# A hybrid attention layer: the differential mixer's output normalized on VectorE, its heads 2 and 3 written in place

## The chip, the cores and the metric

One NeuronCore of one Trainium2 chip runs the whole kernel. The metric is the device time of one execution in microseconds (us). Engines: PE is TensorE (matmul), DVE is VectorE, ACT is ScalarE, POOL is GpSimd, SP is the sync engine, which issues all DMAs here.

## What is computed

One layer on a sequence of 1024 tokens of 1024 features, all in float32. The normalized input is projected to queries, keys and values of two mixers; both mixers' outputs (8 rows of 128 features) are concatenated and projected back; then come a gated convolutional FFN, a gated per-layer input and a last norm. The change is in the second mixer and in the output projection behind it. Cut to that:

```python
for blk in range(s // Q_BLOCK):            # 8 blocks of 128 queries, for each of 4 heads
    sc = einsum('bqhmd,bkhmd->bhmqk', q[:, qs:qe], k[:, :qe]) * HEAD_DIM ** -0.5
    sc = where(allowed, sc + bias, NEG_INF)   # keys up to the block's end: 128, 256, ... 1024
    pr = softmax(sc)
    a = pr[:, :, 0] - lam * pr[:, :, 1]       # two maps m = 0, 1 a head
    outs.append(einsum('bhqk,bkhe->bqhe', a, v[:, :qe]))
o = rms_norm(concatenate(outs), subln_g) * (1.0 - lambda_init)
h = h + concatenate([oa, ob]) @ w_out
```

## The kernel before

Every operand of a matmul is held as a high part and a low part (tensor minus high part), and each product is three matmuls (`SPLIT3`). ACT writes the high part, then DVE writes the low part by a subtraction (`low`, L781; on the profile's lines L513 and L783).

The stages follow one another: input norm and value projection, seven units of the query and key projection, mixer A with further units between its blocks (to 214 us), mixer B, `oproj`, FFN, last stage. All engines run hand-written streams in program order, held together by semaphores.

**Mixer B** is 32 blocks, m = 8 times head plus query block; m mod 8 = i gives a width of w = 128(i + 1) keys. The loop over n (L1292 on PE, L637 on ACT, L976 on DVE, L480 on POOL) is a software pipeline: in turn n, PE issues

- the scores of block n (`b_score`, L1223), after the exponentials of block n-1 (they share their PSUM banks);
- the product with the values of block n-2 (L1295), after its low part (`b_tlo`);
- in turns 28 to 34 a `c_unit`;
- the turn of the finished output of block n-3 (L1317, PSUM bank 7), after `b_y` and after `b_part` of block n-2, which uses the same bank;
- the turn of the probabilities of block n-1 (L1325), after their difference (`b_diff`);
- a filler: half of a projection unit (12 matmuls of 512 columns), in turns 1 to 20. Two halves make a unit, whose result ACT and DVE split (`unit_hi`, `unit_lo`), and which now and then is followed by the split of a further weight tile;
- from turn 26 on a `c_unit` at the end: 9 matmuls that apply `C_ROWS` = 3 of the 8 rows of `w_out` to one half tile of the output; DVE adds it to h (`c_add`, L917).

ACT in turn n: `b_part` of n-2 (L645: both halves of the product, 256 columns, from PSUM, scaled), the copy of the turned output of n-3 (`b_yhi`), the high part of the turned probabilities of n-1 (`b_thi`), the two exponentials of n (`b_exps`, L583), the square of the output of n-2 (L665), then `fill_hi` and `wo_hi` (split of rows of `w_out`).

DVE in turn n: the difference of n-1 (`b_diffs`, L883), the logits of n (`b_logits`, L896: a minimum over the keys farther than 256, then two bias-and-minimum passes), `b_ylo` of n-3, `b_tlo` of n-1, `fill_lo`, `wo_low`, with `c_add` between.

POOL per block (L480 to L494): adds the halves of the product, takes the power of the mean square, scales the output (L491), multiplies by the gain (L494, `b_y`).

SP writes each of the 32 turned outputs to DRAM (`mix_b`) and reads them back as rows 4 to 7 of `act_t`; it also loads `w_out`, mixer A's rows and the residual. After turn 34 PE waits for all 16 `c_unit`s to be added and for `b_ylo` of block 31, and runs `oproj` (L1354) with the 5 remaining rows for 8 tiles.

```python
                pe.wait_ge(S.b_y, m + 1)                     # L1313, m = n - 3
                pe.wait_ge(S.b_part, min(m + 2, NBS))
```

Of the kernel before, what the change touches and what calls it, by code (L numbers as in the profile page):

```python
# [63 lines left out]
def build(nc, x, p, w_in, w_out, sinks, lambda_q, lambda_k, subln_gain, rel_bias, norm_mix, norm_ffn,  # L64
# [57 lines left out]
    y_t = bias_a[:, 0, 0, :]  # L122
# [26 lines left out]
    wp = wbuf[:, 6 * D:10 * D].rearrange("p (l k n) -> p l k n", l=2, k=KP)  # L149
    pt = wbuf[:, 0:D].rearrange("p (s l n) -> p s l n", s=2, l=2)  # L150
# [8 lines left out]
    b_scores b_max b_exp b_diff b_turned b_thi b_tlo b_pv b_part b_sum b_sq b_y b_yturned b_yhi b_ylo  # L159
    wo_hi wo_lo mix_c mix_3 mix_456 mix_7 c_done c_added oproj h_mid sq1 ms1 pow1 xs1_ready tr1 xhi1 xlo1 gffn_in  # L160
# [44 lines left out]
    C_TWO = C_FROM + 2 * (NBS + 3 - C_FROM) - 2 * NT  # L205

    def c_mid(n):
        return C_TWO - C_FROM + 2 * (n - C_TWO) if n >= C_TWO else None

    def c_end(n):  # L210
        return c_mid(n) + 1 if n >= C_TWO else n - C_FROM if n >= C_FROM else None

    def c_bank(c):
        return c % 2 if c > c_mid(NBS) else 0


    WO_SPLITS = {24: (0,), 25: (1, 2), NBS: (3,), NBS + 1: (4, 5), NBS + 2: (6,)}
# [47 lines left out]
    def _(sp):  # L265
# [97 lines left out]
        def load_wo(k):  # L363
            if k >= 3:
                sp.wait_ge(S.wo_lo, k - 2)
            sp.dma_start(raw[:, k % 3, :], w_out[k * P:(k + 1) * P, :]).then_inc(raw_loaded[k % 3], 16)

        for n in range(NBS):
# [5 lines left out]
            if n == 18:  # L374
                sp.wait_ge(S.a_pv, NA)
                sp.wait_ge(S.unit_done, NUNIT)
                for k in range(3):
                    load_wo(k)
            if n == 19:
                sp.wait_ge(S.a_stored, 16 * NA)  # L380
                mix_a_back(0, S.mix_c)
                mix_a_back(1, S.mix_c)
            if n == 20:
                mix_a_back(2, S.mix_c)
                sp.wait_ge(S.w_lo, NTILE)
# [69 lines left out]
        sp.wait_ge(b_stored[0], 16 * (NBS // 2))  # L455
        sp.wait_ge(b_stored[1], 16 * (NBS // 2))
# [3 lines left out]
    def _(pool):  # L460
# [19 lines left out]
        for n in range(NBS):  # L480
            o, st = o_t[:, :], 16 + 3 * (n % 2)
            pool.wait_ge(S.b_part, n + 1)
            if n >= 1:
                pool.wait_ge(S.b_y, n)
            nc.gpsimd.tensor_tensor(o, o_sb[:, 0, :], o_sb[:, 1, :], ALU.add).then_inc(S.b_sum, 1)
            pool.wait_ge(S.b_sq, n + 1)
            link(nc.gpsimd.tensor_scalar(stat[:, st + 1:st + 2], stat[:, st:st + 1], 1.0 / P, EPS, ALU.mult, ALU.add))
            link(nc.gpsimd.tensor_tensor(stat[:, st + 2:st + 3], stat[:, st + 1:st + 2], stat[:, 63:64], ALU.pow))
            if n == 0:
                pool.wait_ge(S.consts_scaled, 1)  # L490
            link(nc.gpsimd.tensor_scalar(o, o, stat[:, st + 2:st + 3], None, ALU.mult))  # L491
            if n >= 1:
                pool.wait_ge(S.b_yturned, n)
            nc.gpsimd.tensor_tensor(y_t[:, :], o, g_sub[:, :], ALU.mult).then_inc(S.b_y, 1)  # L494
# [16 lines left out]
    def _(act):  # L511
# [984 lines left out]
```

## Time and profile before

| what | value |
|---|---|
| median of 3 runs | 1411.56 us (1409.98 to 1412.71) |
| the profiled execution's own time | 1411.1 us |
| its span, first to last instruction | 1409.3 us |
| mean granted TensorE clock | 0.979 |
| PE busy | 1325.0 us (94%) |
| DVE, ACT, POOL busy | 801.3, 405.7, 127.9 us |
| mixer B, first score to last turn | 205 to 458 us of the span |
| `oproj` | 458.6 to 527 us |

A busy share is that of the whole span. Where the order of the streams matters, the timeline is the view to read: it lists instructions of one or all engines in order of time, with the idle time before each and what ended it.

### The profile page before, as it was taken

How to read it: one execution, taken by the hardware profiler on the slowest of the kernel's cores; microseconds unless marked ns; L12 is line 12 of the kernel's file. 1: busy time of each engine (PE TensorE's matmuls, PEld its weight loads, DVE VectorE, ACT ScalarE, POOL GpSimd, SP SyncE). 2: the span in 40 equal slices, each digit the busy share in tenths (PEclk: the TensorE clock that was granted, in tenths of full speed). 3: DMA queues.
4: the chain of work that ended last, by engine and by line, in shares of the span. 5: the costliest groups of instructions: out<-in, count | busy, mean ns of one | idle time of the engine just before them, and what ended most of it. 6: DMA issues, size and time to landing. Idle time of an engine off the chain costs nothing.

```text
span 1409.3 us, 17050 instructions
## 1 busy us (share of the span) xinstructions
PE 1325.0 (94%) x6451; PEld 1074.7 (76%) x6451; DVE 801.3 (57%) x1316; ACT 405.7 (29%) x792; POOL 127.9 (9%) x205
## 2 busy tenths in 40 slices
PE   4999998888689999999999999999999999979997
PEld 4987876666567787888888888888888888857775
DVE  3424776675575453555666666666556655584443
ACT  4323655554343222111111111111221111123321
POOL 0000002434343000000000000000000000040000
PEclk9999999999689999999999999999999999999999
DMA  6462331100745312111111111111111112121111
GB/s 186 83 113 45 83 83 42 49 19 20 179 138 160 113 31 72 52 56 46 45 45 45 45 45 45 45 45 45 45 45 45 45 46 69 57 90 48 42 38 45
DMA packets 107453, 91.11 MB, mean 65 GB/s; under 512 B 12818, under 2 KB 96522, under 8 KB 107338
## 3 DMA queue, kind: packets, MB, share of 16 engines
q1 hardware_dynamic: 107402, 90.43, 23.0%
q8 instruction: 33, 0.54, 0.2%
q14 instruction: 18, 0.15, 0.0%
HBM read 74.49 MB, written 14.94 MB: 63 GB/s over the span
## 4 chain that ended last, share of the span: by engine, by line
PE 63%; DVE 3%; issue 2%; ACT 1%; POOL 0%; POOLq 0%; ACTq 0%; DVEq 0%
PE ps L1143 62%; DVE h L1068 1%; PE ps L1153 1%; DVE wbuf L783 1%; DVE xs L1099 0%; POOL o_t L491 0%; ACT wbuf L513 0%; DVE conv L1041 0%; DVE conv L1051 0%; DVE conv L1046 0%; PE ps L1412 0%; DVE h L921 0%; DVE gel L1134 0%; ACT L768 0%; DVE conv L1122 0%
## 5 line engine op out<-in xcount | busy, mean ns | idle before, releaser
L1143 PE MATMUL ps<-act_t,wbuf 128*128 128x512 f32 x2496 | 592.2, 398 | 6.0 <-DVE wbuf L783 3.7
L1143 PEld LDWEIGHTS ps<-act_t,wbuf 128*128 128x128 f32 x2496 | 470.3, 189 | 123.3 <-DVE wbuf L783 8.1
L1068 DVE TENSOR_TENSOR h<-ps,h 128x512 f32<-128x512 f32 x352 | 238.4, 690 | 199.7 <-PE ps L1143 199.7
L1143 PE MATMUL ps<-wbuf 128*128 128x512 f32 x1152 | 271.4, 393 | 8.8 <-DVE h L1068 8.8
L1143 PEld LDWEIGHTS ps<-wbuf 128*128 128x128 f32 x1152 | 216.8, 189 | 56.7 <-DVE h L1068 10.1
L1143 PE MATMUL ps<-act_t,wq 128*128 128x512 f32 x624 | 157.1, 404 | 0.8 <-DVE wq L785 0.7
L1143 PEld LDWEIGHTS ps<-act_t,wq 128*128 128x128 f32 x624 | 115.8, 191 | 26.8 <-issue 1.1
L783 DVE TENSOR_TENSOR wbuf<-raw,wbuf 128x1024 fp32r<-128x1024 f32 x75 | 87.9, 1220 | 41.4 <-ACT wbuf L678 34.0
L714 ACT ACTIVATE gel<-conv 128x1024 f32<-128x1024 f32 x22 | 23.3, 1060 | 293.1 <-DVE conv L1051 293.1
L513 ACT ACTIVATE a_buf<-ps 128x1024 f32<-128x1024 f32 x22 | 22.6, 1028 | 267.0 <-PE ps L1143 267.0
L1143 PE MATMUL ps<-wbuf,act_t 128*128 128x512 f32 x336 | 85.9, 407 | 3.1 <-DVE h L921 3.0
L499 POOL TENSOR_TENSOR act_t<-raw,act_t 128x1024 fp32r<-128x1024 f32 x6 | 16.7, 2797 | 720.8 <-ACT act_t L513 720.8
L1143 PEld LDWEIGHTS ps<-wbuf,act_t 128*128 128x128 f32 x336 | 62.6, 191 | 18.7 <-DVE h L921 4.6
L678 ACT ACTIVATE wbuf<-raw 128x1024 fp32r<-128x1024 f32 x66 | 64.8, 1044 | 0.0
L1143 PE MATMUL ps<-wq,act_t 128*128 128x384 f32 (+1 forms) x384 | 59.5, 315 | 0.3 <-DVE act_t L783 0.3
L1143 PEld LDWEIGHTS ps<-wq,act_t 128*128 128x128 f32 x384 | 57.8, 193 | 0.7 <-DVE act_t L783 0.7
L783 DVE TENSOR_TENSOR a_t<-ps,a_t 128x512 fp32r<-128x512 f32 (+4 forms) x64 | 44.6, 716 | 22.7 <-ACT a_t L513 22.3
L1143 PE MATMUL ps<-wq 64*128 64x512 f32 (+3 forms) x288 | 38.1, 391 | 14.0 <-ACT e_t L592 13.6
L592 ACT ACTIVATE e_t<-ps,small 128x128 f32<-128x128 f32 (+7 forms) x64 | 46.7, 738 | 5.7 <-DVE small L908 5.6
L1143 PEld LDWEIGHTS ps<-wq 64*128 64x128 f32 x288 | 25.8, 203 | 28.6 <-ACT e_t L592 14.6
L513 ACT ACTIVATE a_t<-ps 128x512 fp32r<-128x512 f32 (+4 forms) x64 | 38.0, 618 | 31.7 <-DMA mix_a<-a_t 12.9
L1143 PEld LDWEIGHTS ps<-v_b,a_t 128*128 128x128 f32 x288 | 40.0, 213 | 8.1 <-issue 5.8
(120 smaller groups left out, 1083.4 us busy)
## 6 DMA issues: line engine op xcount, KB each, us to landing
raw<-in_w_ffn_in SPq DMA_DIRECT2D x44, 512.0 KB, 5.0
raw<-in_w_ffn_out SPq DMA_DIRECT2D x22, 512.0 KB, 5.8
w_raw<-in_w_in SPq DMA_DIRECT2D x10, 512.0 KB, 4.6
x_in<-in_x SPq DMA_DIRECT2D x8, 512.0 KB, 3.3
mix_a<-a_t SPq DMA_DIRECT2D x16, 256.0 KB, 3.0
mix_b<-mst SPq DMA_DIRECT2D x32, 128.0 KB, 1.7
raw<-in_w_out SPq DMA_DIRECT2D x8, 512.0 KB, 5.1
act_t<-mix_a SPq DMA_DIRECT2D x16, 256.0 KB, 5.1
```

Of the source, the lines that this page charges most:

```text
L499: nc.gpsimd.tensor_tensor(act_t[:, 1, r, :], raw[:, (KD + r) % 3, :], act_t[:, 0, r, :].bitcast(F32), ALU.subtract).then_inc(S.wg_lo, 1)
L513: nc.scalar.activation(dst, src, ACT.Copy, scale=scale).then_inc(done, 1)
L592: nc.scalar.activation(e_t[:, pr, m, 0:w], psf[:, at:at + w], ACT.Exp, scale=-1.0, bias=small[:, o + 2 + m:o + 3 + m], accum_out=small[:, ...
L678: ins = nc.scalar.activation(wf[:, s, 0, j, :], raw[:, j, :], ACT.Copy)
L714: nc.scalar.activation(gel[:, :], conv[:, :], ACT.Gelu).then_inc(S.gelu_done, 1)
L783: ins = nc.vector.tensor_tensor(dst, src, hi.bitcast(F32), ALU.subtract)
L1068: nc.vector.tensor_tensor(h[:, t, sl], ps[:, 4 + g % 4, :], h[:, t, sl], ALU.add).then_inc(S.h_add, 1)
L1143: return nc.tensor.matmul(dst, lhs, rhs, start=start, stop=stop)
L1153: ins = nc.tensor.transpose(psf[:, bank * HALF + k * P:bank * HALF + (k + 1) * P], src[:, k * P:(k + 1) * P], ident[:, :])
```

## The change

It moves work and order in mixer B, and rows between the two parts of the output projection:

- the output of a block is no longer scaled and multiplied by the gain on POOL. ACT copies and scales one half of the product to `o_t` (`b_half`), DVE adds the other half in one pass (`b_part`), ACT squares the sum, POOL only computes the power (`b_pow`), and DVE applies power and gain in one pass (`y`, one turn later);
- on ACT, `b_thi` now serves block n-2 and stands first, `b_yhi` serves n-4, and the half of the product of n-2 and its square stand behind the exponentials of n. On DVE, `b_tlo` of n-2 and `b_ylo` of n-4 stand first, then the difference of n-1, the logits of n, y of n-3, `b_part` of n-2;
- on PE the turn of the probabilities of n-1 stands ahead of the turn of the output of n-3, whose waits are the same; the filler follows, in turns 0 to 19; there are 36 turns;
- heads 2 and 3 (blocks 16 to 31) are written straight into `act_t` and not by way of DRAM;
- `C_ROWS` is 2: a `c_unit` has 6 matmuls, stands at the end of the turn, one in turns 22 to 31, two in turns 32 to 34; `oproj` has 6 rows a tile. `w_out` is split in another order, and some tiles lie elsewhere in memory.

```diff
     def b_fill(n):
-        return NA + 1 + n if 1 <= n < HALVES - NA - 1 else None
+        return NA + 2 + n if n < HALVES - NA - 2 else None
-    C_ROWS = 3
-    C_FROM = 26
+    C_ROWS = 2
+    C_FROM = 22
+    VIA_DRAM = 2 * NT
+    def c_units(n):
+        if n < C_FROM:
+            return ()
+        if n < NBS:
+            return (n - C_FROM,)
+        first = NBS - C_FROM + 2 * (n - NBS)
+        return tuple(c for c in (first, first + 1) if c < 2 * NT)
-    WO_SPLITS = {24: (0,), 25: (1, 2), NBS: (3,), NBS + 1: (4, 5), NBS + 2: (6,)}
+    O_ROWS = (4, 5, 6, 2, 3, 7)
+    WO_ORDER = (0, 1) + O_ROWS
+    WO_SPLITS = {20: (0,), 21: (1,), 25: (2,), 26: (3,), NBS: (4,), NBS + 2: (5,), NBS + 3: (6,)}
...
+        sp.wait_ge(S.unit_done, NUNIT)
+        mix_a_back(0, S.mix_c)
+        mix_a_back(1, S.mix_c)
...
+        for j in range(3, KD):
+            load_wo(j)
+            if j == 5:
+                sp.wait_ge(S.c_done, 2 * NT)
+                mix_a_back(2, S.mix_23)
+                mix_a_back(3, S.mix_23)
...
         for n in range(NBS):
-            o, st = o_t[:, :], 16 + 3 * (n % 2)
-            pool.wait_ge(S.b_part, n + 1)
-            if n >= 1:
-                pool.wait_ge(S.b_y, n)
-            nc.gpsimd.tensor_tensor(o, o_sb[:, 0, :], o_sb[:, 1, :], ALU.add).then_inc(S.b_sum, 1)
+            st = 16 + 3 * (n % 2)
             pool.wait_ge(S.b_sq, n + 1)
+            if n >= 2:
+                pool.wait_ge(S.b_y, n - 1)
             link(nc.gpsimd.tensor_scalar(stat[:, st + 1:st + 2], stat[:, st:st + 1], 1.0 / P, EPS, ALU.mult, ALU.add))
-            link(nc.gpsimd.tensor_scalar(o, o, stat[:, st + 2:st + 3], None, ALU.mult))
-            nc.gpsimd.tensor_tensor(y_t[:, :], o, g_sub[:, :], ALU.mult).then_inc(S.b_y, 1)
...
-        for n in range(NBS + 3):
+        for n in range(NBS + 4):
             if 2 <= n <= NBS + 1:
                 m = n - 2
-                nc.scalar.activation(o_sb[:, :, :], ps[:, 7, 0:2 * P].rearrange("p (a q) -> p a q", a=2), ACT.Copy,
-                                     scale=small[:, col:col + 1]).then_inc(S.b_part, 1)
...
                 copy(a_t[:, 0, 0:w], psf[:, 5 * HALF:5 * HALF + w], S.b_thi)
+            if n >= 4:
+                m = n - 4
+                act.wait_ge(S.b_yturned, m + 1)
+                copy(mix_dst(m, 0), ps[:, 7, 3 * P:4 * P], S.b_yhi)
             if 2 <= n < NBS:
                 b_exps(n)
             if 2 <= n <= NBS + 1:
                 m = n - 2
+                act.wait_ge(S.b_pv, m + 1)
+                if m >= 1:
+                    act.wait_ge(S.b_part, m)
+                act.wait_ge(S.b_diff, m + 1)
+                nc.scalar.activation(o_t[:, :], ps[:, 7, 0:P], ACT.Copy,
+                                     scale=small[:, col:col + 1]).then_inc(S.b_half, 1)
+                act.wait_ge(S.b_part, m + 1)
+                square(o_sb[:, m % 2, :], sq_out, stat[:, 16 + 3 * (m % 2):17 + 3 * (m % 2)], S.b_sq)
             fill_hi(b_fill(n))
...
+        for n in range(NBS + 4):
+            if 2 <= n <= NBS + 1:
+                m = n - 2
                 w = P * (m % NT + 1)
                 dve.wait_ge(S.b_thi, m + 1)
                 low(a_t[:, 1, 0:w], psf[:, 5 * HALF:5 * HALF + w], a_t[:, 0, 0:w], S.b_tlo)
+            if n >= 4:
+                m = n - 4
+                dve.wait_ge(S.b_yhi, m + 1)
+                low(mix_dst(m, 1), ps[:, 7, 3 * P:4 * P], mix_dst(m, 0), S.b_ylo)
+            if 2 <= n <= NBS:
+                b_diffs(n - 1)
+            if 2 <= n < NBS:
+                b_logits(n)
+            if 3 <= n <= NBS + 2:
+                m = n - 3
+                dve.wait_ge(S.b_pow, m + 1)
+                nc.vector.scalar_tensor_tensor(out=y_t, in0=o_sb[:, m % 2, :], scalar=stat[:, st + 2:st + 3],
+                                               in1=g_sub[:, :], op0=ALU.mult, op1=ALU.mult).then_inc(S.b_y, 1)
+            if 2 <= n <= NBS + 1:
+                m = n - 2
+                dve.wait_ge(S.b_half, m + 1)
+                nc.vector.scalar_tensor_tensor(out=o_sb[:, m % 2, :], in0=ps[:, 7, P:2 * P],
+                                               scalar=small[:, col:col + 1], in1=o_t[:, :],
+                                               op0=ALU.mult, op1=ALU.add).then_inc(S.b_part, 1)
             fill_lo(b_fill(n))
+            for c in c_units(n):
+                c_add(c)
...
                 ins.then_inc(S.b_turned, 1)
+            if 3 <= n <= NBS + 2:
+                m = n - 3
+                pe.wait_ge(S.b_y, m + 1)
+                pe.wait_ge(S.b_part, min(m + 2, NBS))
+                if m >= 1:
+                    pe.wait_ge(S.b_ylo, m)
+                nc.tensor.transpose(ps[:, 7, 3 * P:4 * P], y_t, ident[:, :]).then_inc(S.b_yturned, 1)
             if b_fill(n) is not None:
                 unit(FIRST_UNITS + b_fill(n) // 2, b_fill(n) % 2)
-            if c_end(n) is not None:
-                c_unit(c_end(n))
+            for c in c_units(n):
+                c_unit(c)
```

## Rows read from the trace of the kernel before

**Rows 1.** Busy time by stretch: us, PE, PEld, DVE, ACT, POOL, PE clock, DMA.

```profile
300.00:340.00 40.00, 35.21 (x212) 27.47 (x211) 24.57 (x62) 20.64 (x60) 16.50 (x30) 1.00 0.06 20
380.00:420.00 40.00, 32.36 (x165) 24.78 (x166) 25.90 (x62) 19.00 (x55) 17.27 (x27) 0.77 0.40 137
```

**Rows 2.** Timeline of all engines, turn 14 (start, us, instruction, idle before).

```profile
301.20 1.49 PE L1143 MATMUL ps<-wq 64*128 64x512 f32 x12
301.64 1.02 DVE L892 SCALAR_TENSOR_TENSOR e_t<-e_t,small 128x768 f32<-128x768 f32 x1
302.62 1.36 PE L1143 MATMUL ps<-v_b,a_t 128*128 128x256 f32 x10
302.76 1.49 DVE L903 TENSOR_REDUCE small<-ps 128x2 f32<-128x1280 f32 x1
303.18 0.61 POOL L491 TENSOR_SCALAR o_t<-o_t,stat 128x128 f32<-128x128 f32 x1
...
304.02 0.47 ACT L645 ACTIVATE o_sb<-ps,small 128x256 f32<-128x256 f32 x1 [2.59 <-PE ps L1143]
304.29 0.49 DVE L908 CUSTOM_DVE_ANT_0 ps<-ps,bias_b,small 128x256 f32<-128x256 f32 x1
...
304.60 0.30 PE L1317 MATMUL ps<-ident,bias_a 128*128 128x128 f32 x1 [0.61 <-POOL bias_a L494]
...
304.73 0.83 PE L1325 MATMUL ps<-ident,e_t 128*128 128x128 f32 x6
...
305.32 3.05 PE L1143 MATMUL ps<-act_t,wq 128*128 128x512 f32 x12
305.60 0.81 ACT L513 ACTIVATE a_t<-ps 128x768 fp32r<-128x768 f32 x1 [0.39 <-PE ps L1325]
306.31 1.00 ACT L592 ACTIVATE e_t<-ps,small 128x896 f32<-128x896 f32 x1
306.45 0.96 DVE L783 TENSOR_TENSOR a_t<-ps,a_t 128x768 fp32r<-128x768 f32 x1 [0.92 <-ACT a_t L513]
...
308.44 1.65 PE L1143 MATMUL ps<-wq 64*128 64x512 f32 x12
...
308.57 0.60 ACT L513 ACTIVATE wq<-ps 128x512 fp32r<-128x512 f32 x1
...
309.20 0.69 DVE L785 SCALAR_TENSOR_TENSOR wq<-ps,wq 128x512 fp32r<-128x512 f32 x1 [1.79 <-ACT wq L513]
```

**Rows 3.** Groups of instructions, whole span: busy us, mean ns of one, idle before.

```profile
L1317 PE MATMUL ps<-ident,bias_a 128*128 128x128 f32 x32 | 10.1, 316 | 19.2 <-POOL bias_a L494 11.2 <-issue 7.3 <-ACT o_sb L645 0.7
L783 DVE TENSOR_TENSOR mst<-ps,mst 128x128 fp32r<-128x128 f32 x32 | 9.2, 287 | 12.8 <-ACT mst L513 12.2
L516 ACT ACTIVATE o_sb<-o_t 128x128 f32<-128x128 f32 x32 | 10.0, 312 | 0.0
```

**Rows 4.** Timeline of PE: turns 1, 3, 21 and 26, and the start of `oproj`.

```profile
217.65 0.47 PE L1325 MATMUL ps<-ident,e_t 128*128 128x128 f32 x1 [2.89 <-DVE e_t L892]
217.78 4.52 PE L1143 MATMUL ps<-act_t,wq 128*128 128x512 f32 x12
...
226.36 0.97 PE L1143 MATMUL ps<-wq 64*128 64x512 f32 x6
...
347.31 1.32 PE L1143 MATMUL ps<-wq 64*128 64x512 f32 x12
...
394.30 2.91 PE L1143 MATMUL ps<-wbuf,act_t 128*128 128x512 f32 x6
...
458.61 21.52 PE L1143 MATMUL ps<-wbuf,act_t 128*128 128x512 f32 x90 [0.85 <-DVE h L921]
```

**Rows 5.** Timeline of all engines after the last exponential (block 31).

```profile
436.15 0.21 ACT L592 ACTIVATION_READ_ACCUMULATOR e_t<-ps,small 128x1 f32 x1
...
452.03 2.71 POOL L491 TENSOR_SCALAR o_t<-o_t,stat 128x128 f32<-128x128 f32 x1
```

**Rows 6.** The page's DMA issues: size of each, median us from issue to landing.

```profile
act_t<-mix_a SPq DMA_DIRECT2D x16, 256.0 KB, 5.1
```

More of the change, by code:

```diff
@@ L361, in residual, with load_wo @@
             sp.dma_start(h[:, t, :], x[t * P:(t + 1) * P, :]).then_inc(x_again[t], 16)
[L363 to L368, printed above, removed]
+        def load_wo(j):
+            k = WO_ORDER[j]
+            if j >= 3:
+                sp.wait_ge(S.wo_lo, j - 2)
+            sp.dma_start(raw[:, j % 3, :], w_out[k * P:(k + 1) * P, :]).then_inc(raw_loaded[j % 3], 16)
+        for n in range(VIA_DRAM):
             sp.wait_ge(S.b_ylo, n + 1)
@@ L677, in f_split_hi @@
                     continue
[L678 removed]
+                ins = nc.scalar.activation(wf[:, 1 - s, 0, j, :], raw[:, j, :], ACT.Copy)
             ins.then_inc(S.f_hi, 1)
@@ L887, in b_diffs @@
             dve.wait_ge(S.b_exp, 2 * m + 2)
+            if m >= 2:
+                dve.wait_ge(S.b_part, m - 1)
             link(nc.vector.reciprocal(small[:, o + 12:o + 14], small[:, o + 8:o + 10]))
@@ L974, in _ @@
                 b_logits(1)
-        for n in range(NBS + 3):
-            if 2 <= n <= NBS:
-                b_diffs(n - 1)
-            if n > C_FROM:
-                c_add(c_end(n - 1))
-            if 2 <= n < NBS:
-                b_logits(n)
-            if c_mid(n) is not None:
-                c_add(c_mid(n))
-            if 3 <= n:
-                m = n - 3
-                dve.wait_ge(S.b_yhi, m + 1)
-                low(mst[:, m % 2, 1, 0:P], ps[:, 7, 3 * P:4 * P], mst[:, m % 2, 0, 0:P], S.b_ylo)
-            if 1 <= n <= NBS:
-                m = n - 1
+        for n in range(NBS + 4):
+            if 2 <= n <= NBS + 1:
+                m = n - 2
                 w = P * (m % NT + 1)
@@ L1290, in _ @@
                 unit(FIRST_UNITS + a_fill(n) // 2, a_fill(n) % 2)
-        for n in range(NBS + 3):
+        for n in range(NBS + 4):
             if 2 <= n < NBS:
@@ L1308, in _ @@
                 ins.then_inc(S.b_pv, 1)
-            if c_mid(n) is not None:
-                c_unit(c_mid(n))
-            if n >= 3:
-                m = n - 3
-                pe.wait_ge(S.b_y, m + 1)
-                pe.wait_ge(S.b_part, min(m + 2, NBS))
-                if m >= 1:
-                    pe.wait_ge(S.b_ylo, m)
-                nc.tensor.transpose(ps[:, 7, 3 * P:4 * P], y_t[:, :], ident[:, :]).then_inc(S.b_yturned, 1)
             if 1 <= n <= NBS:
@@ L1364, in oproj @@
                         ins = mm(ps[:, 2 * (t % 2) + half, :], act_t[:, a, k, t * P:(t + 1) * P],
-                                 wo(k)[:, b, HALF * half:HALF * (half + 1)],
-                                 k == C_ROWS and n == 0, k == KD - 1 and n == 2)
-            if rows[-1] == KD - 1:
+                                 wo(k, b)[:, HALF * half:HALF * (half + 1)],
+                                 k == O_ROWS[0] and n == 0, k == O_ROWS[-1] and n == 2)
+            if rows[-1] == O_ROWS[-1]:
                 ins.then_inc(S.oproj, 1)
```

182 lines of the change are left out of this document (75 added, 107 removed).

## The prediction

> **What bounds the kernel now.** I read the busy time by stretch first. In a stretch of mixer B with fillers PE is busy 35.2 of 40 us at the full clock of 2.4 GHz; later, without fillers, it is busy 32.4 of 40 us at a granted 0.77, part of it at the lower level of 1.2 GHz [rows 1]. Then the timeline of one turn, 14 (i = 6), says what closes the loop. From one score to the next are 7.24 us (301.20 to 308.44), and PE works in almost all of it: score, product, 0.61 us idle, output turn, probability turn, 3.05 us of filler, 0.1 us idle [rows 2]. Beside it DVE takes the difference, the minimum and the logits, and ACT the two exponentials, which end just as the filler does. So the logits and exponentials of a block are hidden under PE's product, turn and filler of the same turn. That overlap is what the change has to be read against. FFN and last stage run as before; I give them no change.
>
> **The change, part by part.** Call e(n) the end of the exponentials of block n.
>
> *The turn of the output now ends behind the exponentials.* PE's turn of output n-3 still waits for `b_part` of n-2, and the filler stands behind it. Before, ACT made `b_part` first thing in the turn (304.02, then the turn at 304.60) [rows 2]. Now it comes from ACT's half copy, queued behind the exponentials of n, and from DVE's pass. So PE has its score, its product and the probability turn, and then nothing until e(n). After e(n): the half copy takes between 0.31 us (128 columns from SBUF) [rows 3] and 0.47 us (256 columns from PSUM) [rows 2], I take 0.38; the pass on DVE between 0.29 [rows 3] and 0.49 [rows 2], I take 0.38; with 0.1 us between engines and 0.13 for the turn (304.60 to 304.73) the filler starts at e(n) + 1.0 and ends at e(n) + 4.05 [rows 2]. Only then does score n+1 start; it used to start at e(n).
>
> *Even turns.* e(n+1) = 4.05 + score + minimum + first logit pass and its reading + exponentials. Means over the eight widths: score 1.08 (0.97 at i = 3 [rows 4], 1.49 at i = 6 [rows 2]); minimum 0.83 (1.49 at 1280 columns, some 0.13 less for each 128, none in two of eight blocks); first pass 0.70 (0.49 and the read of its result); exponentials 1.58 (306.31 to 308.44 is 2.13 at 896 columns, 0.22 less for each 128) [rows 2]. Sum with gaps 8.3 us.
>
> *Odd turns* finish a projection unit. ACT converts it (0.60) and DVE after that (0.69), both behind the filler that ends at e(n) + 4.1; and behind them, in both queues, stand the copies of the probabilities of n-1, on DVE then the low part of output n-3, then the difference of n, then the logits of n+1. Chain: 4.1 + 0.60 + 0.69 + 0.05 + low part 0.76 (0.96 at 768 columns [rows 2], 0.29 at 128 [rows 3]) + 0.26 + difference 1.26 (0.44 for the two small operations ahead of it, 301.20 to 301.64, and 0.82 by the same slope from 1.02) + 0.83 + 0.70 + 1.58 = 10.8 us. The high copy of the probabilities (0.81 at 768) runs beside DVE's 0.69. Three weight tiles are split in such turns, some 1.5 us more each.
>
> *Eighteen turns, e(2) to e(20):* 9 pairs of 8.3 + 10.8, and 4.5, are 176.4 us. Before they took 120.95 us (226.36 to 347.31) [rows 4]: **+55.5**. POOL's add, scaling and gain are gone from the path, but the wait that they ended was 19.2 us over all 32 output turns [rows 3], and it is replaced by a longer one.
>
> *The clock.* A wait of 2.89 us before a turn was followed by a filler at 4.52 us in place of 3.05, the lower level for part of it [rows 4, 2]. In wide blocks the new wait ahead of the output turn is minimum + pass + exponentials + 1.0, less product and probability turn: for i = 6, 5.3 less 2.0, over 3 us. I count 14 of 18 turns with such a filler: **+20.5** (1.47 each). Ends: 0 if the clock holds, and 57 if it never recovers (6 such matmuls took 2.91 us at the lower level [rows 4], a filler then 5.8, and the scores double).
>
> *Turns 21 to 31.* A turn with a small `c_unit` (1.45 for 6 matmuls at the 0.239 of `oproj` [rows 4]) chains the same way: 1.0 + 1.45 + 0.1 + addition 0.69 (512 columns, as the unit's low part) + 0.76 + 0.26 + 1.26 + 0.83 + 0.70 + 1.58 = 8.6, 9.1 for these wider eleven; turns 20 and 21 have no `c_unit`, but four rows of `w_out` are split on the way: 103 us. Before: 347.31 [rows 4] to 436.36 [rows 5], 89: **+14**, and **+12** for 8 of 10 `c_units` at the lower level (2.91).
>
> *The end of mixer B.* Before 22.3 us from the last exponential to `oproj` [rows 4, 5]. Three more turns now carry value product, half, pass, output turn, two `c_units` and their additions one behind the other, and a fourth brings the last low part; I take 27 at the full clock and 3 for the lower level: **+5 +3**. The writes past DRAM gone from SP's queue were off the path.
>
> *`oproj`.* One row moves here from the `c_units`: 8 tiles x 6 matmuls x 0.239 (21.52 over 90) [rows 4]: **+11.5**. Ahead of row 2 SP now waits for the last `c_unit`, reads mixer A's rows back (5.1 us to land [rows 6]), then loads two rows of `w_out`, each split in some 2.3 us; under it lie the first 36 matmuls, 8.6 us. Between 0 and 10; taken at **+3**.
>
> *The start.* Filler 0 fills the 2.89 us wait and spares the slow filler, 4.4 us, for one filler more ahead of turn 2: **-1.3** [rows 4].
>
> Sum: 55.5 + 20.5 + 14 + 12 + 5 + 3 + 11.5 + 3 - 1.3 = +123 us on the profiled execution's 1411.1 us, which stands 0.5 us under the median shown: 1534 us.
>
> *POOL against DVE.* The scaling on POOL took 0.61 us in turn 14 [rows 2] and 2.71 us at 452.03 [rows 5]. The Trainium skill, page "SBUF — State Buffer", section "Who interferes with whom", says that a GpSimd operation and a DVE one with two SBUF inputs block each other for the whole instruction; that speaks for the change, since POOL keeps only two one-column operations. By that alone the sum would be at most the 11.2 us that the output turns waited for POOL [rows 3], downward. It would give the fast rival below; the sum doesn't use it, because the path has left POOL.
>
> **The rivals.**
> - *Clock holds.* Same chains, no low fillers: 1534 less 20.5, 12 and 3 is 1498 us. For it: waits of 0.6 to 1 us in mixer B did not lower the clock [rows 1]. Against: the new waits are as long as that of 217.65. 0.15.
> - *Clock mostly down.* 57 in place of 20.5: 1571 us. Each turn still has filler, score and product nearly back to back, which should lift it. 0.09.
> - *Only the output turn binds.* The odd turns cost as the even ones, because the unit's conversion finds room: 18 x 8.3 is 149, +28 in place of 55.5, at the full clock: 1471 us. ACT's and DVE's order speaks against it. 0.08.
> - *Faster.* `b_part` of n-2 comes while PE still has work, so that nothing waits for it. Place: ACT's half copy ahead of PE's output turn. It decides if the exponentials of n end before PE reaches that turn, that is if minimum, pass and exponentials (4.3 at i = 6) are shorter than product and probability turn (2.0). Then the 19.2 us ahead of the output turns [rows 3] go and the moved matmuls add nothing: 1392 us. Only in the narrowest blocks can that hold. 0.04.
> - *Nothing moves:* the filler hides what it did: 1411 us. 0.01.
>
> **How the numbers follow.** The forecast keeps 0.63, and 1534 is its value. Its own terms may be off by some 25 us: clock, the end, the last loads. The range takes in the rival with the full clock and nearly the one with the low clock: 1488 to 1566. A measurement here can tell 0.2% (2.8 us) from no change: faster 0.04, same 0.01, slower 0.95.
>
> **What would show it.** In the profile after, PE should stand idle some 2 to 4.5 us ahead of nearly every output turn, released by DVE's `b_part` pass; score to score from 8 to 16 should take some 78 to 92 us, against the 7.24 us a turn of turn 14; wide even blocks should come 12 us after an odd turn; fillers of about 4.5 us should alternate with 3.05; DVE's low parts of the probabilities should wait for ACT behind the unit's conversion; `oproj` should have 108 matmuls ahead of its third tile's end in place of 90. I am wrong if score n+1 starts at the end of the exponentials of n, if the busy share of PE in 300 to 340 stays near 88%, or if the granted clock there is 1.00 and the time is still above 1520.

## The result and the profile after

The changed kernel takes 1522.12 us (median of 4 runs, 1515.38 to 1524.02) against 1411.22 us before: ratio 1.0775, 95% interval 1.0763 to 1.0788. A turn with a number is a pass of the loop; the turn of an output or of probabilities is a transposition on PE. The forecast was 1534 us in a range of 1488 to 1566. The profiled execution took 1524.02 us with a span of 1522.2. The page of the changed kernel, its span, busy times and granted clock in 40 slices:

```profile
span 1522.2 us, 17036 instructions
PE 1365.8 (90%) x6451; PEld 1103.5 (72%) x6451; DVE 815.3 (54%) x1380; ACT 399.9 (26%) x792; POOL 58.5 (4%) x109
PEclk9999997778857789999999999999999999999999
```

POOL's busy time falls from 127.9 to 58.5 us, as meant. PE issues as many instructions as before, is busy some 41 us longer, and the clock dips over nine slices (7, 7, 7, 8, 8, 5, 7, 7, 8), where before there were two (6, 8). The busy time by stretch puts the loss in its places. The stretches of the changed kernel are cut at the score of turn 3, the score of turn 21, the last exponential, the start of `oproj` and the last transposition in it (L1162, at 640.99) (columns as in [rows 1]):

```profile
226.47:419.77 193.30, 132.46 (x618) 101.73 (x618) 85.55 (x223) 60.88 (x176) 13.28 (x36) 0.79 0.11 32
419.77:526.14 106.37, 68.96 (x329) 52.07 (x328) 59.33 (x142) 37.20 (x101) 8.12 (x22) 0.70 0.26 82
526.14:558.66 32.52, 21.80 (x84) 17.56 (x85) 13.44 (x24) 6.68 (x17) 2.21 (x6) 0.74 0.02 5
558.66:640.99 82.33, 79.52 (x369) 64.31 (x370) 33.79 (x35) 19.71 (x27) 4.38 (x8) 1.00 0.29 75
640.99:1522.00 881.01, 857.50 (x3713) 691.89 (x3711) 503.74 (x596) 178.74 (x199) 25.42 (x22) 0.99 0.16 50
```

The kernel before, cut at the same instructions:

```profile
226.36:347.31 120.95, 105.07 (x632) 81.56 (x631) 77.88 (x188) 64.55 (x174) 47.84 (x90) 1.00 0.09 29
347.31:436.36 89.05, 69.51 (x375) 54.99 (x374) 55.54 (x121) 39.62 (x102) 33.71 (x55) 0.79 0.53 147
436.36:458.61 22.25, 18.77 (x90) 14.62 (x88) 11.63 (x17) 6.51 (x15) 10.51 (x14) 0.92 0.62 178
458.61:526.70 68.09, 68.09 (x320) 55.41 (x321) 33.78 (x35) 19.73 (x27) 4.39 (x8) 1.00 0.24 71
526.70:1409.00 882.30, 858.89 (x3713) 692.93 (x3711) 503.71 (x596) 178.73 (x199) 25.40 (x22) 0.99 0.16 50
```

So +72.4 in the turns with fillers, +17.3 in turns 21 to 31, +10.3 at the mixer's end, +14.2 in `oproj`; what lies before and after these takes 1.2 us less. In the first stretch PE's idle time goes from 15.9 to 60.8 us (+45.0) and its busy time from 105.1 to 132.5, though one filler (3.05 us) has moved out of it: the same matmuls take some 30 us longer at a granted 0.79.

Turn 14 of the changed kernel, timeline of all engines, to be laid beside [rows 2]:

```profile
350.70 1.49 PE L1152 MATMUL ps<-wq 64*128 64x512 f32 x12
...
353.20 1.33 PE L1152 MATMUL ps<-v_b,a_t 128*128 128x256 f32 x10 [1.02 <-DVE mst L779]
...
354.49 0.88 PE L1325 MATMUL ps<-ident,e_t 128*128 128x128 f32 x6
...
356.54 1.01 ACT L586 ACTIVATE e_t<-ps,small 128x896 f32<-128x896 f32 x1 [4.37 <-DVE small L906]
...
357.54 1.00 ACT L586 ACTIVATE e_t<-ps,small 128x896 f32<-128x896 f32 x1
...
358.52 0.36 ACT L656 ACTIVATE o_t<-ps,small 128x128 f32<-128x128 f32 x1
358.92 0.35 DVE L1000 SCALAR_TENSOR_TENSOR o_sb<-ps,small,o_t 128x128 f32<-128x128 f32 x1 [1.89 <-ACT o_t L656]
...
359.37 0.30 PE L1334 MATMUL ps<-ident,bias_a 128*128 128x128 f32 x1 [4.00 <-issue]
...
359.50 4.58 PE L1152 MATMUL ps<-act_t,wq 128*128 128x512 f32 x12
...
364.01 1.66 PE L1152 MATMUL ps<-wq 64*128 64x512 f32 x12
```

Score to score is now 13.3 us (350.70 to 364.01), where it was 7.24. PE has ended the probability turn at 355.4 and stands still for 4.00 us. What it waits for is read from the ends of the rows ahead: second exponential to 358.5, ACT's half to 358.9, DVE's pass to 359.27, output turn at 359.37. The filler behind it then takes 4.58 us in place of 3.05, and only when it is done does the next score start, although the exponentials which that score waited for ended 5.5 us before.

The groups of the whole span (busy, mean ns, idle before) and the costliest wait of ACT in mixer B (us in all, times, longest):

```profile
L1334 PE MATMUL ps<-ident,bias_a 128*128 128x128 f32 x32 | 12.5, 389 | 75.4 <-issue 71.2 <-DVE o_sb L1000 2.9 <-DVE bias_a L994 1.3
ACT e_t L586 <- DVE small L906: 156.8, 32, 7.6
```

The idle time ahead of the output turns went from 19.2 [rows 3] to 75.4 us, and ACT stands idle 156.8 us ahead of the exponentials, waiting for logits, where it was 5.7 us before. PE has a second new wait, ahead of the product with the values, for DVE's low parts; the groups of the kernel before and of the changed one:

```profile
L1143 PE MATMUL ps<-v_b,a_t 128*128 128x256 f32 x144 | 42.7, 375 | 0.3 <-DVE a_t L783 0.3
L1152 PE MATMUL ps<-v_b,a_t 128*128 128x256 f32 x144 | 46.5, 400 | 30.8 <-DVE mst L779 15.0 <-DVE act_t L779 14.8 <-DVE a_t L779 1.0
```

### The profile page after: what moved, and what is told of

Its sections match the earlier page's. It is cut to its first block, busy times and chain, and to the rows that moved or that the text cites. A ratio compares the mean times of both kernels' runs of the same rounds, so it can differ in the third digit from the quotient of the medians.

```text
span 1522.2 us, 17036 instructions
## 1 busy us (share of the span) xinstructions
PE 1365.8 (90%) x6451; PEld 1103.5 (72%) x6451; DVE 815.3 (54%) x1380; ACT 399.9 (26%) x792; POOL 58.5 (4%) x109
## 4 chain that ended last, share of the span: by engine, by line
PE 79%; DVE 9%; issue 7%; ACT 2%; DMA 1%; SPq 1%; POOL 0%; POOLq 0%; ACTq 0%; DVEq 0%
PE ps L1152 76%; DVE small L901 2%; PE ps L1162 1%; DVE a_t L779 1%; DVE wbuf L779 1%; DVE h L1077 1%; PE ps L1334 1%; ACT wq L507 1%; DVE ps L906 1%; DMA raw<-in_w_out 0%; PE ps L1325 0%; SPq L284 0%; DMA mix_a<-a_t 0%; ACT e_t L586 0%; DVE act_t L779 0%
## 5 line engine op out<-in xcount | busy, mean ns | idle before, releaser
L1152 PE MATMUL ps<-act_t,wq 128*128 128x512 f32 x624 | 179.0, 446 | 1.6 <-DVE wq L781 1.5
L1152 PEld LDWEIGHTS ps<-act_t,wq 128*128 128x128 f32 x624 | 132.0, 217 | 32.9 <-issue 2.0
L586 ACT ACTIVATE e_t<-ps,small 128x128 f32<-128x128 f32 (+7 forms) x64 | 46.8, 736 | 156.8 <-DVE small L906 156.8
L1334 PE MATMUL ps<-ident,bias_a 128*128 128x128 f32 x32 | 12.5, 389 | 75.4 <-issue 71.2
L1152 PE MATMUL ps<-v_b,a_t 128*128 128x256 f32 (+1 forms) x288 | 48.9, 326 | 30.8 <-DVE mst L779 15.0
L1152 PE MATMUL ps<-wbuf,act_t 128*128 128x512 f32 x288 | 69.2, 397 | 5.0 <-issue 2.2
L1152 PEld LDWEIGHTS ps<-v_b,a_t 128*128 128x128 f32 x288 | 44.4, 233 | 39.8 <-DVE a_t L779 35.9
L1152 PEld LDWEIGHTS ps<-wbuf,act_t 128*128 128x128 f32 x288 | 53.5, 188 | 18.7 <-issue 4.1
L1334 PEld LDWEIGHTS ps<-ident,bias_a 128*128 128x128 f32 x32 | 5.5, 171 | 82.1 <-issue 80.3
L779 DVE TENSOR_TENSOR a_t<-ps,a_t 128x512 fp32r<-128x512 f32 (+4 forms) x64 | 44.6, 714 | 17.8 <-ACT a_t L507 17.6
```

What stands on the lines that cost most here:

```text
L586: nc.scalar.activation(e_t[:, pr, m, 0:w], psf[:, at:at + w], ACT.Exp, scale=-1.0, bias=small[:, o + 2 + m:o + 3 + m], accum_out=small[:, ...
L779: ins = nc.vector.tensor_tensor(dst, src, hi.bitcast(F32), ALU.subtract)
L1152: return nc.tensor.matmul(dst, lhs, rhs, start=start, stop=stop)
L1334: nc.tensor.transpose(ps[:, 7, 3 * P:4 * P], y_t, ident[:, :]).then_inc(S.b_yturned, 1)
```

## The experiments

Theory A (the prediction's): `b_part` and what stands behind it come after the exponentials, and the filler and the next score stand behind the output turn that waits for `b_part`; a slower clock follows from the wait. Rivals: only the output turn binds; the clock is the main loss; the gain or loss comes from another part of the change (normalization on DVE, filler 0, early exponentials, `C_ROWS`). All ratios are to the kernel before on the same chip, with their 95% intervals.

**a_fill_first**: the changed kernel, PE's filler and `c_units` ahead of the output turn.

```diff
+            if b_fill(n) is not None:
+                unit(FIRST_UNITS + b_fill(n) // 2, b_fill(n) % 2)
+            for c in c_units(n):
+                c_unit(c)
             if 3 <= n <= NBS + 2:
                 m = n - 3
...
-            if b_fill(n) is not None:
-                unit(FIRST_UNITS + b_fill(n) // 2, b_fill(n) % 2)
-            for c in c_units(n):
-                c_unit(c)
```

> The changed kernel (1522 us) with one edit on PE: the filler and the small c_unit of a turn stand ahead of the turn of the output, not behind it. Theory (PE's turn of the output waits for b_part, which stands behind the exponentials on ACT, and holds back filler and next score): the 3.05 us of filler run inside the wait, score n+1 starts 1.0 us after the exponentials of n, and the eighteen turns with filler are left to ACT's and DVE's chain of some 7.5 us a turn, 135 us in place of 202 (score 3 to score 21); whole time 1435 to 1455 us. Rival (the added DVE and ACT operations of a turn are what costs, wherever PE waits): less than 15 us gained, above 1505 us.

Measured: 1448.2 us, ratio 1.0265 (1.0235 to 1.0295): 74 us back. The timeline of its turn 14, and its group of the output turns:

```profile
316.83 3.06 PE L1152 MATMUL ps<-act_t,wq 128*128 128x512 f32 x12
...
320.63 0.35 DVE L1000 SCALAR_TENSOR_TENSOR o_sb<-ps,small,o_t 128x128 f32<-128x128 f32 x1 [1.89 <-ACT o_t L656]
...
321.08 0.30 PE L1338 MATMUL ps<-ident,bias_a 128*128 128x128 f32 x1 [1.19 <-issue]
...
321.31 1.65 PE L1152 MATMUL ps<-wq 64*128 64x512 f32 x12
```

```profile
L1338 PE MATMUL ps<-ident,bias_a 128*128 128x128 f32 x32 | 9.7, 303 | 26.3 <-issue 26.0
```

The chain to the output turn is the same, and PE spends it in the filler, at 3.06 us: the wait of 4.00 becomes 1.19, and the score follows the turn at once. From score 3 to score 21 pass 139.8 us (193.3 in the changed kernel). Taking the filler out from behind the wait gives back two thirds of the loss, the slower clock that came with the wait included.

**a_half_first**: the changed kernel, ACT's half copy and square ahead of the exponentials.

```diff
-            if 2 <= n < NBS:
-                b_exps(n)
             if 2 <= n <= NBS + 1:
                 m = n - 2
...
+            if 2 <= n < NBS:
+                b_exps(n)
```

> The changed kernel with one edit on ACT: the half copy of output n-2 stands ahead of the exponentials of n; DVE's order stays. Theory: b_part then ends just behind the logits, some 2 us ahead of the end of the exponentials, so filler and next score start 2 us earlier in each turn: 35 to 50 us gained, 1472 to 1487 us. Rival (what holds the turn is DVE's chain, not PE's wait): under 10 us.

Measured: 1465.8 us, ratio 1.039 (1.0359 to 1.042): 56 us back, more than expected. Its group, and its turn 14:

```profile
L1336 PE MATMUL ps<-ident,bias_a 128*128 128x128 f32 x32 | 11.3, 353 | 38.8 <-DVE bias_a L996 34.2 <-issue 3.2 <-DVE o_sb L1002 1.4
```

```profile
329.95 0.35 DVE L996 SCALAR_TENSOR_TENSOR bias_a<-o_sb,stat,g_sub 128x128 f32<-128x128 f32 x1
330.21 0.34 DVE L1002 SCALAR_TENSOR_TENSOR o_sb<-ps,small,o_t 128x128 f32<-128x128 f32 x1
330.65 0.45 PE L1336 MATMUL ps<-ident,bias_a 128*128 128x128 f32 x1 [2.03 <-DVE bias_a L996]
```

The wait halves and changes its releaser. The label names DVE's `y` (L996); in turn 14 `y` ends at 330.30, DVE's pass right behind it at 330.55, and the output turn starts 0.1 us later. Both stand behind the logits on DVE. So a copy that is early on ACT alone doesn't restore the old time: what is left of the loss is 55 us.

**a_conv_late**: the changed kernel, a unit's conversion put one turn later, ahead of the exponentials on ACT and behind the logits on DVE, so that the probability's copies don't wait for it.

```diff
+            if n >= 1:
+                fill_hi(b_fill(n - 1))
...
-            fill_hi(b_fill(n))
```

> The changed kernel, but ACT and DVE convert a finished projection unit one turn later, where they have slack: on ACT ahead of the exponentials, on DVE behind the logits. Theory of two chains: an odd turn then costs what an even one does, 2.5 us less in 9 turns and 1.5 us less in the 3 with a weight split, 27 us, and less of the lower clock: 1485 to 1500 us. Rival (only the turn of the output binds, the conversion finds room): 1517 to 1525 us.

Measured: 1494.25 us, ratio 1.0591 (1.056 to 1.0622): 28 us back, all of it in turns 3 to 20 (162.9 against 193.3 us from score 3 to score 21). The conversion in odd turns was on the path. "Only the output turn binds" had it that the conversion finds room: it falls. The gains of the three runs sum to 158 us, more than the 111 lost: they overlap, as links of one loop do, and are not separate losses.

**a_warm**: the changed kernel with work added: in six of the eight widths 12 to 22 identity turns per block on PE, ahead of the turn of the probabilities and into the place that it writes, to keep PE busy in what was the wait.

```diff
+                if 3 <= n < NBS:
+                    for z in range(WARM[n % NT]):
+                        nc.tensor.transpose(psf[:, 5 * HALF:5 * HALF + P], ident[:, :], ident[:, :])
                 pe.wait_ge(S.b_diff, m + 1)
```

> The changed kernel with 12 to 22 more 128x128 turns of the identity a turn on PE in turns 3 to 31 of widths over 256, written where the turned probabilities go right after; they lie in PE's wait and nobody waits for them. It tells the share of the clock: theory, the granted clock in mixer B rises to over 0.95 and fillers go back to 3.05 us, and the time falls by the 35 us that the prediction put on the clock, to 1487 us (1480 to 1500). Rival: PE's clock is off the path and the time stays within 5 us of 1522; or the waits are too short for them and it grows.

Measured: 1496.14 us, ratio 1.0605 (1.0574 to 1.0635): 26 us back with more work than before. Busy time by stretch, and PE's timeline in turn 12, then the filler of turn 12 in the changed kernel:

```profile
300.00:340.00 40.00, 32.32 (x213) 26.68 (x212) 21.04 (x54) 13.41 (x39) 2.97 (x8) 0.96 0.14 38
```

```profile
318.39 2.92 PE L1326 MATMUL ps<-ident 128*128 128x128 f32 x16
...
322.75 3.06 PE L1153 MATMUL ps<-act_t,wq 128*128 128x512 f32 x12
```

```profile
335.21 5.05 PE L1152 MATMUL ps<-act_t,wq 128*128 128x512 f32 x12
```

The granted clock in 300 to 340 rises from 0.79 to 0.96 and this filler takes 3.06 us in place of 5.05. So the lower clock costs at least 26 us and is a consequence of the waits. 85 us stay, so it isn't the main loss; how much of them is still clock (0.87 in 380 to 420) is open.

**b_late**: the kernel before, with only the order changed: `b_part` and `b_yhi` behind the exponentials, probabilities turned first.

```diff
+            if 2 <= n < NBS:
+                b_exps(n)
             if 2 <= n <= NBS + 1:
                 m = n - 2
...
-            if 2 <= n < NBS:
-                b_exps(n)
```

> The kernel before, with nothing of the change but its order: ACT's b_part and b_yhi stand behind the exponentials, and on PE the turn of the probabilities stands ahead of the turn of the output. Normalization stays on POOL, c_units and DRAM as before. Theory (the order costs, not the operations): score n+1 starts behind the filler, pairs of turns take some 18.2 us in place of 13.4, with the clock and the later turns 1475 to 1500 us. Rival (the work moved to DVE and ACT costs): within 10 us of 1411 us.

Measured: 1489.55 us, ratio 1.0555 (1.0533 to 1.0576). With POOL, filler 0, `C_ROWS` and DRAM as before, the order alone makes the loop and 79 of the 111 us (idle 82.8 us ahead of the turns):

```profile
L1327 PE MATMUL ps<-ident,bias_a 128*128 128x128 f32 x32 | 11.8, 368 | 82.8 <-issue 79.4 <-ACT o_sb L654 2.7 <-POOL bias_a L494 0.7
```

**b_swap**: the kernel before; only the two turns of PE change places, and ACT's and DVE's copies with them; `b_part` stays first.

```diff
-            if n >= 3:
-                m = n - 3
-                pe.wait_ge(S.b_y, m + 1)
...
             if 1 <= n <= NBS:
...
                 ins.then_inc(S.b_turned, 1)
+            if n >= 3:
+                m = n - 3
+                pe.wait_ge(S.b_y, m + 1)
```

> The kernel before with the turn of the probabilities ahead of the turn of the output on PE, and ACT's and DVE's copies in the same order. It takes the one part of the changed order that should help: the 0.61 us that PE waits for b_part in most turns then lies under the turn of the probabilities. Theory: 5 to 15 us gained, 1397 to 1406 us. Rival (the exponentials end no earlier and PE only waits for them instead, at the next score): within 3 us of 1411.

Measured: **1401.07 us** (1400.02 to 1402.5), ratio 0.9927 (0.991 to 0.9943): 0.7% faster than before, with the whole interval below 1. Its group of the output turns, then PE's timeline in turn 14 and at the start of `oproj`:

```profile
L1327 PE MATMUL ps<-ident,bias_a 128*128 128x128 f32 x32 | 9.9, 310 | 3.4 <-issue 2.3 <-POOL bias_a L494 1.1
```

```profile
303.75 0.83 PE L1318 MATMUL ps<-ident,e_t 128*128 128x128 f32 x6
304.53 0.30 PE L1327 MATMUL ps<-ident,bias_a 128*128 128x128 f32 x1
304.59 3.05 PE L1143 MATMUL ps<-act_t,wq 128*128 128x512 f32 x12
...
450.54 21.51 PE L1143 MATMUL ps<-wbuf,act_t 128*128 128x512 f32 x90 [0.85 <-DVE h L921]
```

The probability turn now lies in the 0.61 us that PE used to wait for POOL [rows 2], and 19.2 us of idle become 3.4. This one part of the change is its gain: 10 us.

**b_dve**: `b_swap` with the normalization on DVE as in the change; POOL keeps the power.

```diff
-            link(nc.gpsimd.tensor_scalar(o, o, stat[:, st + 2:st + 3], None, ALU.mult))
-            nc.gpsimd.tensor_tensor(y_t[:, :], o, g_sub[:, :], ALU.mult).then_inc(S.b_y, 1)
...
+                nc.vector.scalar_tensor_tensor(out=y_t, in0=o_t[:, :], scalar=stat[:, st + 2:st + 3],
+                                               in1=g_sub[:, :], op0=ALU.mult, op1=ALU.mult).then_inc(S.b_y, 1)
```

> The kernel b_swap (1401 us) with the normalization on DVE, that part of the change alone: ACT still copies both halves first in the turn, DVE adds them behind the logits and applies power and gain (y of n-3) first in its turn, POOL only takes the power. Theory (the operations are nearly free, the change's order is what costs): within 6 us of b_swap, 1397 to 1406 us, perhaps a little under it for the 0.7 us a turn that POOL no longer adds to the way of the square. Rival (0.65 us more of DVE a turn lies on the way from exponentials to logits): 18 to 30 turns of 0.35 us or more, 1407 to 1420 us.

Measured: 1405.94 us, ratio 0.9952 (0.9933 to 0.9971), 4.9 us above `b_swap`, at the upper end of what was expected; the intervals overlap, so there is no gain and perhaps a small loss. The same move on PE's old order, where output turns still waited for POOL, was not run.

**b_swap_f0**: `b_swap` with the fillers in turns 0 to 19.

```diff
-        return NA + 1 + n if 1 <= n < HALVES - NA - 1 else None
+        return NA + 2 + n if n < HALVES - NA - 2 else None
```

> b_swap with the fillers in turns 0 to 19 and not 1 to 20, that part of the change alone. Theory: filler 0 fills the 2.89 us wait ahead of the first turn of probabilities and spares the one slow filler of 4.52 us, and one more turn later on is bare: 0 to 4 us gained, 1397 to 1401 us. Rival: the bare turn, at the lower clock, costs more than the start gives, 1402 to 1405 us.

Measured: 1407.78 us, ratio 0.9972 (0.9962 to 0.9982): 6.7 us slower than `b_swap`, beyond both expectations. PE's timeline of `b_swap_f0`, turns 0 to 2, up to the score of 3:

```profile
216.37 3.06 PE L1143 MATMUL ps<-act_t,wq 128*128 128x512 f32 x12 [0.78 <-DVE wq L785]
...
222.28 0.79 PE L1143 MATMUL ps<-wq 64*128 64x384 f32 x6
...
224.83 0.44 PE L1318 MATMUL ps<-ident,e_t 128*128 128x128 f32 x2 [1.38 <-DVE e_t L892]
...
228.01 0.97 PE L1143 MATMUL ps<-wq 64*128 64x512 f32 x6
```

Filler 0 does fill the wait of 2.89 us, and DVE is late one turn after (1.38 us). Score 3 comes at 228.01 and not at 226.37, but 0.84 us of this were there at the score of turn 0, ahead of anything that was moved (206.26 against 205.42). In `b_dve_f0`, below, which has the same fillers, score 2 comes 1.4 us earlier than in `b_swap` (222.22) and score 3 at the same time:

```profile
220.86 0.79 PE L1152 MATMUL ps<-wq 64*128 64x384 f32 x6
...
226.38 0.97 PE L1152 MATMUL ps<-wq 64*128 64x512 f32 x6
```

So at the start the early filler neither gains nor costs. The loss comes later (2.5 us from score 3 to score 21, 2 more to `oproj`); the fillers' conversions now fall in other turns, and whether they do it was not tried.

**b_dve_f0**: both of these on `b_swap`.

```diff
-        return NA + 1 + n if 1 <= n < HALVES - NA - 1 else None
+        return NA + 2 + n if n < HALVES - NA - 2 else None
```

> Both of them together, b_dve and the fillers from turn 0. Theory: the two are independent, so the sum of their differences to b_swap within 1.5 us; 1395 to 1404 us. Rival: they share the same slack and together give no more than one.

Measured: 1412.68 us, ratio 1.0003 (0.9986 to 1.0019), outside what was expected. It is 11.6 us above `b_swap`, and 4.9 + 6.7 is 11.6 too. That the two costs add to the microsecond is not shown: the ten runs lie in two groups, 1408.37 to 1410.67 and 1414.68 to 1416.55, and the median falls between them.

**a_order**: the changed kernel with the order of before on ACT and DVE: both halves copied first by ACT, `b_thi` ahead of the exponentials, `b_tlo` and `b_ylo` behind the logits, the sum on DVE. With the order goes the form of the copy: both halves by ACT, and not one by ACT and one by DVE.

```diff
-            if 1 <= n <= NBS:
-                m = n - 1
...
+                nc.scalar.activation(o_sb[:, :, :], ps[:, 7, 0:2 * P].rearrange("p (a q) -> p a q", a=2), ACT.Copy,
+                                     scale=small[:, col:col + 1]).then_inc(S.b_part, 1)
...
-                nc.scalar.activation(o_t[:, :], ps[:, 7, 0:P], ACT.Copy,
-                                     scale=small[:, col:col + 1]).then_inc(S.b_half, 1)
```

> The changed kernel with everything of it but the order on ACT and DVE: both halves copied by ACT first in the turn, the probabilities of n-1 copied ahead of the exponentials, the output of n-3 turned and copied in the same turn, the sum and y on DVE as in b_dve. Normalization, fillers from 0, heads 2 and 3 in place, small c_units from turn 22, six rows in oproj stay. Theory (order is the whole of the loss in the turns; what is left is oproj's 11.5 us, 3 us of wait for w_out and the c_units' new place): 1400 to 1418 us. Rival (the placement of rows and the writes in place cost on their own): over 1430 us.

Measured: 1420.25 us, ratio 1.0067 (1.005 to 1.0083), 2 us above what the theory said (1400 to 1418). All else of the change is in it, so the order gives back 102 of the 111 us. Its group and the start of its `oproj`:

```profile
L1335 PE MATMUL ps<-ident,bias_a 128*128 128x128 f32 x32 | 9.3, 292 | 3.4 <-DVE bias_a L983 1.7 <-issue 1.4
```

```profile
449.88 8.67 PE L1153 MATMUL ps<-wbuf,act_t 128*128 128x512 f32 x36 [0.85 <-DVE h L921]
461.23 2.16 PE L1153 MATMUL ps<-wbuf,act_t 128*128 128x512 f32 x6 [2.69 <-DMA act_t<-mix_a]
```

It is 19.2 us above `b_swap`. By stretch nearly all of this lies in `oproj`, which takes 85.9 us (449.88 to 535.77) where it takes 68.1 in `b_swap`: 11.4 for the moved row, 3.9 for the two waits (for mixer A's rows and for a split tile of `w_out`), and some 2.5 for matmuls that run slower behind them (6 in 2.16 us and 66 in 17.64). Mixer B ends no later than in `b_swap` (449.88 against 450.54), although `b_dve_f0` says that its normalization and fillers cost there; the `c_units` of `a_order` have 6 matmuls and not 9. `C_ROWS`, the writes in place and the loads were not run one by one.

**b_exps_bare** and **b_exps_all**: `b_swap` with the exponentials of n ahead of the copy `b_thi` of n-1, in turns 21 to 25 (no filler) or in all; `b_part` stays first.

```diff
+            if 21 <= n <= 25:
+                b_exps(n)
...
-            if 2 <= n < NBS:
+            if 2 <= n < NBS and not 21 <= n <= 25:
```

> b_swap (1401 us) with the changed kernel's other idea in the five turns without any filler (21 to 25) only: ACT's exponentials of n ahead of the high copy of the probabilities of n-1. Theory: in a bare turn the next score waits for the exponentials, which wait for PE's turn of the probabilities and its copy; without that wait a wide turn is DVE's and ACT's chain of 7.3 to 8.5 us in place of 8.0 to 10.0: 2 to 6 us gained, 1395 to 1399 us. Rival (the low copies and the difference come later by as much as the exponentials come earlier): 1400 to 1404 us.

> The same order on ACT in all turns. It separates the changed kernel's early exponentials from its late b_part: here b_part stays first. Theory (a turn with filler is bound by PE, and the late copies put thi, tlo, difference and logits in one chain of 7.6 to 8.5 us, longer than PE's 7.2 only in the widest blocks): within 6 us of b_swap, 1397 to 1407 us. Rival (this chain is the real loss in the changed kernel): over 1420 us.

Measured: 1399.46 us, ratio 0.9913 (0.9896 to 0.9929), and 1404.21 us, ratio 0.9953 (0.9935 to 0.997). The first is the lowest time of all, but its interval overlaps that of `b_swap`, and it lies between what theory and rival said. Early exponentials in all turns cost 3 us by the medians (three runs at 1401 to 1402, three at 1407), where the rival had over 1420; it is `b_part` behind them that costs. Every version with `b_part` behind the exponentials is slower than before by 2.7 to 7.8%, and every version with ACT's copy of both halves first is within 0.7% of it or faster. `a_half_first`, whose `b_part` stands behind the logits on DVE, is 3.9% slower.

## Why the prediction was right

**The loop** was as predicted. In turn 14 half and pass took 0.36 and 0.35 us where 0.38 each was taken, and the filler started 0.96 us after the exponentials where 1.0 was said. PE waited ahead of most output turns, 26 of the waits labelled "issue" with 2.7 us each (71.2 over 26), 4.4 at most. From score 8 to score 16 passed 88.9 us (287.84 to 376.74), where 78 to 92 were said. PE's busy share in 300 to 340 fell from 88% to 69% (27.47 of 40 us), and the granted clock there is 0.79, so neither of the two signs of being wrong that name this stretch came. Turns 3 to 20 took 72.4 us more than before; the working had 55.5 for the chain and 20.5 for the clock, 76. The chain was oversized and the clock undersized: the 17 fillers took 23.6 us more than 17 times 3.05, which leaves 49 for all else. That the sum came out nearer than its terms is luck. The exponentials of wide even block 14 ended 13.3 us after those of 13, where 12 was said. `a_fill_first`, `a_half_first` and `a_conv_late` each take one link out, and each link was carrying time.

One sign did not come as worded: DVE's low parts were to wait for ACT behind the unit's conversion. DVE hardly waits longer for ACT there (17.6 us in all ahead of these low parts, 22.3 before); it is PE that now waits for the low parts, 30.8 us ahead of the product with the values. The conversion is on the path all the same, as `a_conv_late` shows.

**The clock** fell a little more than said. Of the 17 fillers of turns 3 to 19, 12 took 4.28 to 5.47 us, one 3.86 and only four 3.04 to 3.16. The count of slow ones was right (14 of 18), their mean is 4.86 us and not 4.52, and they don't alternate with 3.05 but come in rows, turns 3 to 7 and 10 to 15. The rivals "clock holds" (1498) and "clock mostly down" (1571) enclosed the result. The 57 us of the second doesn't follow from its own terms: if the level never rises, all 18 fillers cost 2.75 more and the scores some 19, together 69. `a_warm` shows the cause: with PE kept busy the level stays up in most of the turns.

**Turns 21 to 31** were oversized, +26 against +17.3. PE's busy time there hardly changes (69.5 to 69.0, with 329 matmuls recorded against 375), and its idle time goes from 19.5 to 37.4 us. The exponentials of blocks 20 and 31 end at 418.65 and 526.14 in the trace, 107.5 us apart, where 103 + 12 = 115 were said. The two turns without a `c_unit` were sized too long (18.8 us to the end of the exponentials of 22, where the working has 2 times 9.1 and 3 for the splits). In the other nine, seven `c_units` ahead of a later block's exponentials ran at 2.88 to 2.91 us in place of some 1.64, 9 us where 12 was said; the chain without this took 8.9 us a turn, 9.1 was said.

**The end of mixer B**: +8 forecast, +10.3 measured. It was estimated as a whole, and so is not split here. PE's timeline after the last exponential, with the two longest waits, and at the start of `oproj`, changed kernel:

```profile
531.63 3.22 PE L1152 MATMUL ps<-v_b,a_t 128*128 128x256 f32 x14 [2.14 <-DVE act_t L779]
...
543.37 2.74 PE L1152 MATMUL ps<-v_b,a_t 128*128 128x256 f32 x16 [3.41 <-DVE act_t L779]
...
558.66 8.64 PE L1152 MATMUL ps<-wbuf,act_t 128*128 128x512 f32 x36 [2.23 <-issue]
568.33 1.64 PE L1152 MATMUL ps<-wbuf,act_t 128*128 128x512 f32 x6 [1.02 <-DMA act_t<-mix_a]
...
571.74 15.67 PE L1152 MATMUL ps<-wbuf,act_t 128*128 128x512 f32 x66 [1.78 <-DVE wbuf L779]
```

**`oproj`**: +14.5 forecast, +14.2 measured. The 108 matmuls are there (36, 6 and 66), the moved row is worth 11.4 us (PE's busy time goes from 68.09 to 79.52), and the two waits, for mixer A's rows and for a split tile of `w_out`, sum to 2.8 where 3 was taken.

**The start**: the step "spares the slow filler: -1.3" failed. Score 2 does come 1.5 us earlier (220.76), and score 3 at 226.47, 0.1 later than before. What filler 0 gains, PE then waits for DVE in turn 2 (0.98 us for a low part and 0.34 for the difference, nothing in the kernel before). A filler put into a wait is no gain when DVE is the next that is late. By `b_swap_f0` the moved fillers even cost 6.7 us on a kernel without the long waits, most of it after the start. The terms of the forecast sum to 123 us and the profiled executions differ by 112.9; of the 10 us between, turns 21 to 31 make nearly 9.

**POOL** off the path gave nothing: `b_dve` is 4.9 us above `b_swap`. The prediction named a rule that speaks for this move. The Trainium skill, page "SBUF — State Buffer", section "Who interferes with whom", says that a DVE instruction with two SBUF inputs contends with a GpSimd one that reads SBUF. No run here measures that contention by itself; what the runs say is that most of the 19.2 us ahead of the output turns (all but 3.4) went by reordering, with POOL's work left where it was.

**The faster rival** had named `b_part` as its place, and it was the place: with `b_part` early and the turns exchanged the kernel is faster, 1401.07 us. That rival's 1392 was the whole 19.2 us; 10 of them came.

## What to carry to other kernels

An engine's instructions are a queue: before an operation is moved behind a longer one, list what stands behind its consumer, here the filler and the next score; here the wait grew from 0.61 to 4.00 us and the turn by 6.1, though the moved copy and pass take 0.7 us together. If a filler is to cover a wait, it stands ahead of the waiting instruction; if an engine waits for a short result while it holds other ready work, exchange the two. Undo the order alone first: it gave back 102 of 111 us in one run, and doing a part of the order alone on the old kernel (`b_swap`) showed that one exchange was the useful part of a large change.

## What the runs showed that was not expected

- The wait of an output turn is labelled "issue" (71.2 of 75.4 us), although the turn starts 0.1 us after DVE's pass in turn 14 and moving that pass earlier halves it. A large "issue" ahead of an instruction with a semaphore wait is to be read from the rows that end just ahead of it.
- PE's granted clock followed the waits closely. In 300 to 340 it is 1.00 before, in `b_swap` and in `a_order`, 0.96 in `a_warm`, 0.84 in `b_late` and 0.79 in the changed kernel. Matmul busy time in turns 3 to 20 rose from 105 to 132 us for one filler less, and 16 identity turns in a wait cost 2.92 us of PE and brought the filler behind them back to 3.06 us.
- The runs of the changed kernel spread over 1515.38 to 1524.02 us, with mean granted clocks of 0.951 for the fastest and 0.943 for the profiled one; `b_swap` spread over 1400.02 to 1402.5. The spread goes with the clock in `b_dve_f0` too: its five faster runs have 0.984 to 0.987, the five slower ones 0.978 to 0.981. Why is open.
